# A triangular inverse moved from 128x128 matmuls to 32x32 tiles in the recurrent stage of a decoder step

## The reference

```python
def step(S, inp):
    r_t, w_t, k_t, v_t, kk_t, b_t = inp
    sa = jnp.einsum('bhvk,bhk->bhv', S, kk_t)
    S = S * w_t[:, :, None, :] - sa[..., None] * b_t[:, :, None, :] + v_t[..., None] * k_t[:, :, None, :]
    return S, jnp.einsum('bhvk,bhk->bhv', S, r_t)
```

## Time and profile before

| | |
|---|---|
| median of three runs | 2044.34 us |
| span of the profiled execution | 2043.6 us, instructions 33681 |
| PE busy | 1855.5 us (91%) |
| DVE, ACT, POOL busy | 941.1 (46%), 600.7 (29%), 364.8 us (18%) |
| recurrent stage, loop | about 478 to 1133 us of the span, 8 laps |
| mean granted clock of PE over the span | 0.955 of full speed |

### The profile page before, as it was taken

How to read it: one execution, slowest core, us unless ns; L and a number is a source line. 1 busy time by engine, 2 the same in 40 slices (tenths; PEclk the granted TensorE clock), 3 DMA queues, 4 the chain that set the end, 5 groups by cost and what they waited for, 6 DMA issues and landing times. The chain is left out here.

```text
span 2043.6 us, 33681 instructions
## 1 busy us (share of the span) xinstructions
PE 1855.5 (91%) x13379; PEld 1542.9 (75%) x13379; DVE 941.1 (46%) x1522; ACT 600.7 (29%) x842; POOL 364.8 (18%) x331
## 2 busy tenths in 40 slices
PE   7999999998999999999999899999988887877776
PEld 7999999997787878877888799999967443443332
DVE  6553445547465465664755544555533121112213
ACT  5333232323233133232332533334434111100112
POOL 0640003113120321212203000273032000000002
PEclk9999999999999999999999899999988988988888
DMA  7444344434222131222220543644663999999995
GB/s 278 165 147 176 122 168 168 147 127 134 78 89 94 52 115 64 89 97 69 93 88 21 191 185 134 248 165 182 234 266 151 421 430 431 431 431 432 432 431 236
DMA packets 46599, 409.32 MB, mean 200 GB/s; under 512 B 6580, under 2 KB 8376, under 8 KB 16696
## 3 DMA queue, kind: packets, MB, share of 16 engines
q1 hardware_dynamic: 46520, 408.17, 51.5%
HBM read 396.98 MB, written 11.18 MB: 200 GB/s over the span
## 5 line engine op out<-in xcount | busy, mean ns | idle before, releaser
L380 PE MATMUL ps<-x_high,w_high 128*128 128x288 f32 x928 | 255.6, 302 | 9.7 <-ACT w_high L586 8.9
L381 PE MATMUL ps<-x_rest,w_high 128*128 128x288 f32 x928 | 251.5, 298 | 0.0
L380 PEld LDWEIGHTS ps<-x_high,w_high 128*128 128x128 f32 x928 | 175.7, 189 | 13.2 <-ACT w_high L586 10.5
L381 PEld LDWEIGHTS ps<-x_rest,w_high 128*128 128x128 f32 x928 | 175.7, 189 | 0.5
L542 ACT ACTIVATE w_high<-w_raw 128x2048 fp32r<-128x2048 f32 x57 | 109.2, 1916 | 152.6 <-DMA w_raw<-in_w_main 78.3
L1598 POOL TENSOR_TENSOR xm<-ring,const 128x512 f32<-128x512 f32 x56 | 94.9, 1694 | 306.8 <-DVE ring L1495 221.9
L1108 PE MATMUL ps<-x_high,r_high 128*128 128x288 f32 x512 | 146.1, 310 | 0.0
L653 DVE TENSOR_TENSOR w_rest<-w_raw,w_high 128x2048 fp32r<-128x2048 f32 x58 | 138.8, 2395 | 11.3 <-ACT w_high L542 11.1
L385 PE MATMUL ps<-x_high,w_rest 128*128 128x288 f32 x928 | 132.1, 295 | 1.0 <-DVE w_rest L653 1.0
L1108 PE MATMUL ps<-rx_low,r_high 128*128 128x288 f32 x480 | 130.7, 298 | 0.0
L385 PEld LDWEIGHTS ps<-x_high,w_rest 128*128 128x128 f32 x928 | 126.0, 188 | 1.2 <-DVE w_rest L653 1.2
(11 more groups left out here) (574 smaller groups left out, 4237.5 us busy)
## 6 DMA issues: line engine op xcount, KB each, us to landing
w_raw<-in_w_main SPq DMA_DIRECT2D x57, 1024.0 KB, 4.9
ring<-in_w_g SPq DMA_DIRECT2D x32, 1024.0 KB, 4.8
half_b<-in_w_egu SPq DMA_DIRECT2D x16, 2048.0 KB, 22.5
half_a<-in_w_egu SPq DMA_DIRECT2D x15, 2048.0 KB, 18.2
ring<-in_w_u SPq DMA_DIRECT2D x32, 512.0 KB, 3.5
ring<-in_w_gate SPq DMA_DIRECT2D x8, 2048.0 KB, 7.8
ring<-in_w_out SPq DMA_DIRECT2D x8, 2048.0 KB, 8.3
half_d<-in_w_egu SPq DMA_DIRECT2D x8, 2048.0 KB, 22.5
```

The source lines that it names most:

```text
L380: mm(o, high[:, t % 2, k, :], x_h[:, k, :], start=(k == 0), stop=False)
L381: ins = mm(o, high[:, t % 2, k, :], x_l[:, k, :], start=False, stop=False)
```

## The change

The inverse of the 32x32 diagonal blocks is built first, with the four blocks of each of the four matrices laid side by side: T, U and z shrink from 128x512 to 128x128 (`tc`, `uc`, `zc`), and A's diagonal blocks are copied into `bc`. Level 0 needs no matmul: DVE masks it, turns it with its own transpose of 32x32 blocks and subtracts it from the identity. Levels 1 to 4 run on PE as `forward` (sixteen 32x32 matmuls `z`, then four that turn T into U through the identity, `ub`) and `back` (sixteen 32x32 matmuls `t`); ACT copies `z`, DVE copies the turned U and subtracts `t`. Each of the sixteen lies on its own 32x32 part of the array. The two last levels are done by block: `z5` and `u5` (8 and 12 matmuls of 32x32) join blocks of 32 to blocks of 64, and `z6`, `u6` (four of 64x64 each) join those to 128. The full U of the tail (`um`) is put together from the pieces by ACT and DVE; its lower blocks are set to zero once, by POOL, ahead of the loop.

The fillers are the same work in other places: `G10` 12 to 32 in level 1, `U10` in levels 2 and 3, the rest of `G10` in level 4, `U11` in the two block levels. The sample steps move to PSUM bank 7, `w0` and `w1` to banks 1 and 7 and wait for less. On DVE `rest("10")`, `rest("11")`, the mixes of the next lap and the merge stand at other places. The seven 128-column masks leave the constant tensor and one of 32 and one of 160 columns come in.

The diff, cut to its core:

```diff
+    c["ident_c"] = (s % BLK == t[:, :BLK])
+    c["level_c"] = np.concatenate([np.tile(level[m][:BLK, :BLK], (NBLK, 1)) for m in LEVELS if m < BLK], 1)
...
-        xm = sb("xm", [P, 2, 4, P])
+        xm = sb("xm", [P, NIN, 4, BLK])
+        bc = sb("bc", [P, 4, BLK])
+        tm64 = sb("tm64", [P, 4, 64])
...
-                    pe.wait_ge(v.sem, v.at(("bk01", "bk10")[h], i))
+                    if h == 1:
+                        pe.wait_ge(v.sem, v.at("m01", i))
                     settled(pe)
                     for y in H:
-                        ins = mm(ps[NSM * y:NSM * y + NSM, 4 + h, :], kr[hs(h), y, NPR:T], sts[hs(h), :, :], start=True, stop=True)
+                        ins = mm(ps[NSM * y:NSM * y + NSM, (1, 7)[h], :], kr[hs(h), y, NPR:T], sts[hs(h), :, :], start=True, stop=True)
...
+                def forward(l):
+                    pe.wait_ge(g_.sem, g_.at("x1" if l == 1 else "x2", i))
+                    pe.wait_ge(v.sem, v.at("sk1" if l == 1 else f"t{l - 1}", i))
+                    settled(pe)
+                    for j in range(4):
+                        for n in range(NBLK):
+                            ins = mm(ps[block_(j), 3 + n, 0:BLK], xm[block_(n), l, j, :], tc[block_(n), j, :], start=True, stop=True)
+                    q.done(ins, f"z{l}")
+                    for j in range(4):
+                        ins = mm(ps[block_(j), 2, 0:P], tc[:, j, :], ident, start=True, stop=True)
+                    q.done(ins, f"ub{l}")
+                def back(l):
+                    pe.wait_ge(a.sem, a.at(f"z{l}", i))
+                    pe.wait_ge(v.sem, v.at(f"ub{l}", i))
+                    settled(pe)
+                    for n in range(NBLK):
+                        for j in range(4):
+                            ins = mm(ps[block_(n), 3 + j, 0:BLK], uc[block_(j), n, :], zc[block_(j), n, :], start=True, stop=True)
+                    q.done(ins, f"t{l}")
...
+                forward(1)
+                filler("G10", 12, 22)
+                back(1)
+                pe.wait_ge(v.sem, v.at("wm1", i))
+                pe.wait_ge(g_.sem, g_.at("sx0", i))
+                sample("sz0", lambda h: sxm[:, 0, h, :], lambda h: K("ident", NSM)[:, 0:NSM])
+                filler("G10", 22, 32)
+                forward(2)
...
+                filler("G10", 32, 40)
+                back(4)
+                filler("G10", 40, 48)
+                pe.wait_ge(v.sem, v.at("t4", i))
+                settled(pe)
+                for j in range(4):
+                    for g in range(2):
+                        ins = mm(ps[block_(2 * g + 1), 3 + 2 * g, j * BLK:(j + 1) * BLK], bbm[block_(2 * g), j // 2, j % 2, 0, block_(2 * g + 1)],
+                                 tc[block_(2 * g), j, :], start=True, stop=True)
+                q.done(ins, "z5")
...
+                for j in range(4):
+                    mm(ps[block_(1), 4, j * BLK:(j + 1) * BLK], uc[block_(1), j, :], zc[block_(1), j, :], start=True, stop=True)
+                    for g in range(2):
+                        ins = mm(ps[block_(2 * g), 4 + 2 * g, j * BLK:(j + 1) * BLK], zc[block_(2 * g + 1), j, :], uc[block_(2 * g + 1), j, :],
                                  start=True, stop=True)
+                q.done(ins, "u5")
+                filler("U11", 2, 4)
+                pe.wait_ge(a.sem, a.at("td", i))
+                pe.wait_ge(v.sem, v.at("u5", i))
+                settled(pe)
+                for j in range(4):
+                    ins = mm(ps[64:128, 3, j * 64:(j + 1) * 64], bbm[0:64, j // 2, j % 2, 0, 64:128], tm64[0:64, j, :], start=True, stop=True)
+                q.done(ins, "z6")
+                filler("U11", 4, 6)
+                pe.wait_ge(a.sem, a.at("z6", i))
+                settled(pe)
+                for j in range(4):
+                    ins = mm(ps[0:64, 5, j * 64:(j + 1) * 64], z6[:, j, :], um[64:128, j, 64:128], start=True, stop=True)
+                q.done(ins, "u6")
+                filler("U11", 6, 8)
...
+                for l in range(1, 5):
                     act.wait_ge(q.sem, q.at(f"z{l}", i))
+                    if l > 1:
+                        act.wait_ge(q.sem, q.at(f"t{l - 1}", i))
+                    a.done(fn(zc, ps[:, 3:7, 0:BLK], ACT.Copy), f"z{l}")
+                    if l == 2:
                         act.wait_ge(q.sem, q.at("sz1", i))
+                        a.done(fn(sz[:, :, :], ps[0:NSM, 7, 0:64].rearrange("p (h t) -> p h t", h=2), ACT.Copy), "sz1")
+                    if l == 3:
                         split("11", 0, 8)
+                    if l == 4:
                         split("11", 8, 16)
+                act.wait_ge(v.sem, v.at("t4", i))
+                fn(tm64[block_(0), :, 0:BLK], tc[block_(0), :, :], ACT.Copy)
+                a.done(fn(tm64[block_(1), :, BLK:2 * BLK], tc[block_(1), :, :], ACT.Copy), "td")
+                act.wait_ge(q.sem, q.at("z5", i))
+                fn(zc[block_(1), :, :], ps[block_(1), 3, 0:P].rearrange("p (j t) -> p j t", j=4), ACT.Copy)
+                a.done(fn(zc[block_(3), :, :], ps[block_(3), 5, 0:P].rearrange("p (j t) -> p j t", j=4), ACT.Copy), "z5")
+                act.wait_ge(v.sem, v.at("ua", i))
+                for n in reversed(range(NBLK)):
+                    ins = fn(um[block_(n), :, block_(n)], uc[block_(n), :, :], ACT.Copy)
+                a.done(ins, "ud")
+                act.wait_ge(q.sem, q.at("z6", i))
+                a.done(fn(z6, ps[64:128, 3, 0:256].rearrange("p (j t) -> p j t", j=4), ACT.Copy), "z6")
+                tanh("10")
...
+                bb = bbm[:, :, :, 0, :].rearrange("p h c t -> p (h c) t")
+                W("bk11")
+                for n in range(NBLK):
+                    ins = nc.vector.tensor_copy(bc[block_(n), :, :], bb[block_(n), :, block_(n)])
+                v.done(ins, "bc")
+                W("bc")
+                level = lambda l: K("level_c")[:, l * BLK:(l + 1) * BLK].unsqueeze(1).to_broadcast([P, 4, BLK])
+                v.done(tt(xm[:, 0, :, :], bc[:, :, :], level(0), ALU.mult), "x0")
+                W("x0")
+                v.done(nc.vector.transpose(flat(uc), flat(xm[:, 0, :, :])), "xt")
+                W("xt")
+                v.done(tt(tc, K("ident_c").unsqueeze(1).to_broadcast([P, 4, BLK]), uc, ALU.subtract), "t0")
...
+                decay(0)
+                turned(1)
+                decay(1)
+                updated(1)
+                dve.wait_ge(g_.sem, g_.at("sx0", i))
+                v.done(tt(su[:, :, :], one2, sxm[:, 0, :, :], ALU.subtract), "su0")
+                WQ("sz0")
+                v.done(tt(st_[:, :, :], one2, h2(ps[0:NSM, 7, 0:64]), ALU.subtract), "st0")
+                rest("10", 0, 8)
+                turned(2)
+                rest("10", 8, 16)
+                updated(2)
+                differences("k", 9)
+                mixes("k", k, 9)
+                turned(3)
+                W("us_k")
+                v.done(ts(kk, k, par("k_k", i + 1), None, ALU.mult), "kkr")
+                updated(3)
+                WQ("su1")
+                v.done(tt(su[:, :, :], su[:, :, :], h2(ps[0:NSM, 7, 0:64]), ALU.subtract), "su1")
+                differences("r", 1)
+                turned(4)
+                mixes("r", r, 1)
+                updated(4)
+                W("t4")
+                v.done(nc.vector.transpose(flat(uc), flat(tc)), "ua")
+                scaled("10")
+                WQ("u5")
+                v.done(ts(tm64[block_(1), :, 0:BLK], j4(ps[block_(1), 4, 0:P]), -1.0, None, ALU.mult), "t5")
+                ts(um[block_(0), :, block_(1)], j4(ps[block_(0), 4, 0:P]), -1.0, None, ALU.mult)
+                v.done(ts(um[block_(2), :, block_(3)], j4(ps[block_(2), 6, 0:P]), -1.0, None, ALU.mult), "u5")
+                rest("11", 0, 8)
+                WQ("u6")
+                v.done(ts(um[0:64, :, 64:128], j4(ps[0:64, 5, 0:256]), -1.0, None, ALU.mult), "u6")
+                merge(1, 0)
...
+                pool.wait_ge(v.sem, v.at("bc", i))
+                g_.done(tt(xm[:, 1, :, :], bc[:, :, :], level(1, 1).to_broadcast([P, 4, BLK]), ALU.mult), "x1")
+                def sample_level(l):
+                    g_.done(tt(sxm[:, l, :, :], sk[:, :, 1, 0, :],
+                               K(f"seq_level{LEVELS[l]}", NSM).unsqueeze(1).to_broadcast([NSM, 2, NSM]), ALU.mult), f"sx{l}")
+                pool.wait_ge(v.sem, v.at("sk1", i))
+                sample_level(0)
+                g_.done(tt(xm[:, 2:NIN, :, :], bc[:, :, :].unsqueeze(1).to_broadcast([P, NIN - 2, 4, BLK]),
+                           level(2, NIN - 2).unsqueeze(2).to_broadcast([P, NIN - 2, 4, BLK]), ALU.mult), "x2")
+                sample_level(1)
```

More of the change, by code:

```diff
@@ L955, in stage_rwkv @@
         um = scratch[:, 2048:2560].rearrange("p (j t) -> p j t", j=4)
[L956 to L957 removed]
+        tc, uc, zc = (scratch[:, 2560 + 128 * n:2688 + 128 * n].rearrange("p (j t) -> p j t", j=4) for n in range(3))
+        flat = lambda x: x.rearrange("p j t -> p (j t)")
```

(40 more changed lines are left out.)

181 lines of the change are left out of this document (33 added, 148 removed).

## The result

The changed kernel takes 1955.46 us (median of four runs, 1954.55 to 1959.61) against 2043.91 us (2043.24 to 2045.64): a ratio of 0.9568, 95% interval 0.9554 to 0.9582. The forecast was 1987, so the gain is 88.5 us where 57 was expected. In the two profiled executions the eight laps last 573.5 instead of 661.4 us, which is 87.9 of it; the program reaches its first lap 3.7 us later and is 5.0 us shorter behind the loop.

The account below looks back on a forecast made before the run. PE was taken to bound the kernel. The terms summed to a middle of 25.3 us against 32.4, so 7.1 a lap and 57 in eight laps: 1987 us, own range 1972 to 2001, wider range 1962 to 2028.

Parts of the forecast that it names:

- I take 19, since four tiles are nearer to sixteen than one is: Small 32-column rows of the middle: 19 ns each, from twelve rows on four tiles; 296 rows make 5.6 us.
- The rule on the issue gap: Trainium skill's rule for PE that matmul starts never come closer than about 25 ns, however few the columns.
- What goes: PE work removed from the middle: 18 groups of four 128x128 matmuls a lap, 0.89 us each, 16.0 us.
- Shape changes: Switching tile shapes in the middle: 0.75 us a level, 0.32 a block step; 4.3 us, ends 2.5 and 6.
- Cover at no cost: Other engines' work in the middle stays hidden under PE's fillers, costed at nothing but the entry, 0.1 us.
- Nothing gained: Entry to the middle: `w0` and `w1` wait for less, PE can arrive earlier, but then waits for `sk1`.
- (b): Small tiles run better, 13 ns a row, and shape changes at their low end: gain 86 us, 1958; chance 0.13.
- (a): Small tiles of the middle don't overlap, 31 ns a row: gain 28 us, 2016; chance 0.12.
- (a'): Small tiles of the middle overlap in part, 25 ns a row: gain 42 us, 2002; chance 0.10.
- (c): Chain sticks out: DVE or ACT late by some 0.3 us at ten of fourteen hand-offs, 2011 us; chance 0.12.
- (d): Granted clock dips in the middle with its many small tiles, costing 27 us of the gain: 2014; chance 0.07.
- (e): Clock low for half of the middle: lap 5.5 us longer, slower than before, 2088 us; chance 0.08.

Follow-up runs that it names:

- the undone `z`: Changed kernel with `z` of levels 1 to 4 put back to four 128x128 matmuls, `t` and `ub` kept: 1977.54 us (0.9692).
- the last run: Changed kernel with diagonal tiles, `uc` turned by DVE, `sk` masked first, fillers and sample work moved, POOL's masks waiting for `ub1`: 1945.94 us (0.9526).

## Why the prediction was right or wrong

The direction and the mechanism were right: PE work goes, the fillers stay, the chain stays covered. The size was wrong, by one term above all. The middle by distances between starts in the trace, us a lap:

| term | forecast | measured |
|---|---|---|
| fillers (36 x 0.13, 32 rows x 0.243) | 12.5 | 12.5 |
| samples | 0.9 | 0.6 |
| 296 small rows, first start to last | 5.6 | 1.7 |
| `ub` | 1.0 | 0.7 |
| `z6`, `u6` | 0.9 | 0.9 |
| shape changes (what is left of 21.49) | 4.3 | 5.1 |
| entry | 0.1 | 0.25 |
| sum | 25.3 | 21.7 |

The 3.6 us are 28 in eight laps: 1987 becomes 1959. Most of the other 3.5 us is no term of the sum: I multiplied the steady lap by eight, but in the execution before the first lap was 1.9 us longer (84.26) and the fourth 0.85 (83.17). The 3.7 and 5.0 us outside the loop nearly cancel, and no run says what they are.

**The step that failed** is "I take 19, since four tiles are nearer to sixteen than one is". The run of twelve does lie on four tiles, but L1245 and L1246 share two of them: each of these two takes four rows one behind the other between 705.31 and 705.52, and that alone makes the run so long. The rows that the earlier trace rows leaves out show it:

```profile
705.39 0.23 PE L1245 MATMUL ps<-sk,tok 32*64 32x32 f32 x2
705.41 0.23 PE L1249 MATMUL ps<-const,s0t 32*64 32x32 f32 x2
```

One such tile takes its rows at 705.31, 705.39, 705.45 and 705.51. So the run showed how fast a tile takes its own rows, and I read it as how fast PE hands rows out. It was not even the right tile: these are 32x64, with some 65 ns between a tile's own rows, twice the 31 of a 32x32 tile. The better reading was there too: 31 ns on one 32x32 tile, divided by the tiles in use. The runs show that law at one, two, three and four tiles (30, 16.7, 11, 8.4 ns); for sixteen it gives 2, and the trace has 4.8. My own lower end of 13 came from the first four rows of the same run; these lie on four different tiles, but again on 32x64 ones, and their starts (7 to 14 ns apart in the trace) were no bound for sixteen tiles of 32x32. That made the range too short: it ended at 1962, where 1.7 us for the small rows alone would have given 1956.

**The rule on the issue gap** did not hold across tiles: starts came 5 ns apart, not 25. On the trace's side is another section of the same page that I had not weighed, the Trainium skill ("TensorE: Matmul & The Clock Gate", Part 3: Packing small matmuls), with some 4 ns between starts on different tiles.

**What goes** was right: the undone `z` costs 0.98 us where 0.89 and a change of shape stood.

**Shape changes** came out at 5.1, inside 2.5 to 6. A block step's 0.32 was exact: from 664.19 to 665.73 are 1.54 us, less sixteen rows (0.25) and a filler (0.97) is 0.32. A level takes 1.0 instead of 0.75 (3.60, less 1.94 of fillers, 0.21 of the sample step and 0.47 of rows); 0.25 of it lies between the last start of `t` (659.13) and the sample step (659.38), which have the same tile shape, so the term holds more than changes of shape.

**Cover at no cost** was right: PE waits 0.89 us at the entry, and in all of the middle behind it it is idle for 0.2. The entry was wrong in its cause: I had PE arrive late at 668.6, and it arrives 0.9 us before `sk1`. "Nothing gained" held all the same, since the chain of DVE sets it; moved to `t0`, the wait came back at the sample step.

**Rivals.** (b) came nearest, 1958, though its price a row was still too high. (a) and (a') fall with the pace. (c) does not occur; without cover, three hand-offs cost 1.8 us. (d) and (e): the clock is 1.00 in all laps of the changed kernel while PE works, small tiles or not. The sign "46 ns apart or more" was mis-added: 5.6 and 7.1 us over 296 rows are 43.

**Not in the prediction at all:** the number of PE instructions in a lap. The change raised it from 1194 to 1592, and with 128 more the step took 59 us, two thirds of the gain. No rival had that.

## What to carry to other kernels

Price small matmuls by tile: a tile's own distance, for its own shape, divided by the tiles in use (here down to 4.8 ns a row), and look in a row that seems to show the pace which of its instructions share a tile. Count an engine's instructions in a loop before adding many short ones; here the loss came in one step. When a wait is removed, follow the same chain two steps on, as it was given back at a sample step here, and let an engine that shares a path with the critical one start late.

## What the runs showed that was not expected

- **Code loaded anew.** Up to 1592 PE instructions a lap: 62 instruction packets in the run. From 1720 on: 126 to 134, and a stop of PE of 4.4 to 5.7 us at each turn of the lap, spent in the loop's branch. The Trainium skill ("Runtime: NRT & Kernel Launch", Instruction fetch mechanics) gives PE room for 2048 instructions, filled in blocks of 16 KB. The blocks agree (64 packets more are 1.04 MB); the room does not show as the bound: by the instructions counted in the trace, the step came below 1720.
- **The clock after a stop.** Behind the 4.71 us without PE work the granted clock was 0.50 and then 0.77 for 2 us each; in the laps of the changed kernel, which have no stop, it was 1.00.
- **DVE stands still while POOL works.** A subtraction with both inputs in SBUF took 3.44 us instead of 0.29; in the same lap the transposition at 808.44, one input, ran beside POOL's row at 808.22 in 0.31. The changed kernel has it too: its `su`, two inputs at 652.79, took 0.63 us, to the end of a POOL row (652.55, 0.80 long), and 0.20 in the last run. The Trainium skill ("SBUF — State Buffer", Who interferes with whom) says that a DVE operation with two SBUF inputs contends with a POOL operation that reads SBUF, and that the later one waits in full. The runs agree, and here DVE waited through four POOL operations in a row (804.87 to 808.25).
- **Beyond the first 32 rows of a group** PE was slower: the second sixteen matmuls on sixteen tiles took 0.41 us, the first 0.15. Why was not tried.
